# Second half's layer norm: convolution output turned through DRAM and VectorE instead of TensorE; first half's roots and turned blocks taken earlier

## The reference

```python
z = rmsnorm(x, g_mix) @ w_in            # a | b | v, 512 columns each
u = a * sigmoid(b)
u = causal_depthwise_conv(u, conv_w, conv_b)    # 31 taps, 512 channels
u = silu(layernorm(u, ln_g, ln_b))              # norm over the 512 channels
q = multiscale_pool(v, pool_w, pool_scale)
x = x + concatenate([u, q]) @ w_out
h = rmsnorm(x, g_ffn)                           # then SwiGLU FFN, gated embedding, rmsnorm
```

## Time and profile before

| | us |
|---|---|
| median of 3 runs (lowest, highest) | 990.74 (990.29, 991.52) |
| profiled execution, its own time | 991.45 |
| its span in the trace | 989.6 |
| TensorE busy | 976.5 |
| VectorE busy | 705.1 |
| ScalarE busy | 464.1 |
| GpSimd busy | 392.3 |

### The profile page before, as it was taken

One profiled execution on the slowest core, in us unless ns is written; L12 is line 12 of the kernel. 1 busy time (PEld: TensorE's weight loads), 2 busy tenths in 40 slices (PEclk: granted clock), 3 DMA queues, 4 the chain that ended last, 5 costly groups with the idle time before them and its releaser, 6 DMA issues.

```text
span 989.6 us, 12306 instructions
## 1 busy us (share of the span) xinstructions
PE 976.5 (99%) x4415; PEld 809.3 (82%) x4415; DVE 705.1 (71%) x984; ACT 464.1 (47%) x714; POOL 392.3 (40%) x297
## 2 busy tenths in 40 slices
PE   8999999999999999999999999999999999999996
PEld 7888887888888888888888888888888888888885
DVE  6999989976798365355354454553677888887897
ACT  6726357414364333333423333333444665676865
POOL 3467887920255544544444354451000000012555
PEclk9999999999999999999999999999999999999998
DMA  7631654476625134134233332413999688657432
GB/s 258 139 94 67 125 100 171 169 192 168 194 65 160 54 120 141 58 110 123 87 107 98 116 107 76 137 64 107 352 366 330 238 300 273 193 162 197 152 107 106
DMA packets 175663, 152.94 MB, mean 155 GB/s; under 512 B 73274, under 2 KB 131154, under 8 KB 175602
## 3 DMA queue, kind: packets, MB, share of 16 engines
q1 hardware_dynamic: 174400, 151.76, 49.8%
q10 hardware_dynamic: 1202, 0.40, 0.2%
HBM read 112.02 MB, written 40.11 MB: 154 GB/s over the span
## 4 chain that ended last, share of the span: by engine, by line
PE 81%; DVE 12%; POOL 2%; DMA 2%; ACT 1%; issue 1%; SPq 0%; POOLq 0%; DVEq 0%; ACTq 0%
PE ps L1758 27%; PE ps L1760 27%; PE ps L1759 27%; DVE ps L2226 8%; DMA raw<-in_w_in 2%; PE ps L1809 1%; POOL wide L956 1%; POOL ws_lo L849 0%; DVE resid L2234 0%; DVE resid L2226 0%; DVE ftmp L2655 0%; DVE act_lo L2119 0%; ACT junk L1135 0%; DVE scr L2147 0%; DVE ws_lo L2119 0%
## 5 line engine op out<-in xcount | busy, mean ns | idle before, releaser
L843 POOL TENSOR_SCALAR ss<-ss 128x1 f32<-128x1 f32 x38 | 15.6, 409 | 314.1 <-ACT junk L1135 278.6
L2226 DVE SCALAR_TENSOR_TENSOR ps<-resid,convw,ps 128x512 f32<-128x512 f32 x184 | 123.3, 748 | 0.0
L1758 PE MATMUL ps<-ring_hi,ring_lo 128*128 128x512 f32 x308 | 119.9, 389 | 0.1
L1760 PE MATMUL ps<-ring_hi 128*128 128x512 f32 x308 | 119.8, 389 | 0.0
L1759 PE MATMUL ps<-ring_lo,ring_hi 128*128 128x512 f32 x308 | 119.8, 389 | 0.0
L1758 PE MATMUL ps<-act_hi,bs_lo 128*128 128x512 f32 x240 | 93.5, 389 | 0.0
L1760 PE MATMUL ps<-act_hi,bs_hi 128*128 128x512 f32 x240 | 93.4, 389 | 0.0
L1759 PE MATMUL ps<-act_lo,bs_hi 128*128 128x512 f32 x240 | 93.4, 389 | 0.0
L2421 DVE TENSOR_TENSOR gtmp<-ps,gtmp 128x512 f32<-128x512 f32 x22 | 15.2, 691 | 95.6 <-PE ps L1760 95.6
L1121 ACT ACTIVATE ring_hi<-raw 128x512 fp32r<-128x512 f32 x89 | 51.9, 625 | 60.4 <-PE ps L1760 60.3
L849 POOL TENSOR_TENSOR wc_lo<-raw_b,wc_hi 128x1024 fp32r<-128x1024 f32 x22 | 55.7, 2530 | 48.8 <-ACT wc_hi L1121 47.7
(11 more groups left out here) (293 smaller groups left out, 2668.4 us busy)
## 6 DMA issues: line engine op xcount, KB each, us to landing
raw<-in_w_gate_up SPq DMA_DIRECT2D x44, 512.0 KB, 5.3
raw<-in_scratch SPq DMA_DIRECT2D x52, 256.0 KB, 3.6
raw<-in_w_down SPq DMA_DIRECT2D x52, 256.0 KB, 4.2
in_scratch<-in_s SPq DMA_DIRECT2D x44, 256.0 KB, 3.4
in_scratch<-gtmp SPq DMA_DIRECT2D x33, 256.0 KB, 2.3
keep<-in_w_down SPq DMA_DIRECT2D x32, 256.0 KB, 4.3
keep<-in_scratch SPq DMA_DIRECT2D x25, 256.0 KB, 3.4
resid<-in_x SPq DMA_DIRECT2D x8, 512.0 KB, 7.3
```

Source lines behind the costliest of these rows:

```text
L843: pool.tensor_scalar(ss[:, n:n + 1], ss[:, n:n + 1], 1.0 / D, EPS, ALU.mult, ALU.add)\
L1758: pe.matmul(dst, w_lo_, m_hi, start=start, stop=False, skip_group_check=onto)
L1760: return pe.matmul(dst, w_hi_, m_hi, start=False, stop=stop, skip_group_check=onto)
L2226: dve.scalar_tensor_tensor(out=conv_c if k == last_odd else acc, in0=u_all[:, c, k + h * BANK:k + (h + 1) * BANK], scalar=convw[:, c * 32 ...
```

## The change

The second half takes the first half's way to its layer norm: each chunk is stored to a second scratch tensor, loaded back by blocks, and turned by VectorE (`ln_turn_1`); TensorE's `conv_turn` is gone. The way back (`normed_turn` on TensorE) stays. In SP's queue four stores and eight loads stand between `load_quad(0)` and `store_x1(0)`. VectorE does statistics and scaling two tiles at a time, with `add_x(2)` in between, and scales only when all four tiles are turned, since the scaled tiles overwrite the loaded blocks. In the first half GpSimd takes the roots of tiles 0 and 1 behind the first addition of a window instead of the third, and VectorE's turns of the second pair of normed parts move from unit 6 into unit 5; the low parts `q_low` stand one tap later.

```diff
@@ SP
+            def store_conv_1(j):
+                c = UNIT_C[j]
+                sp.wait_ge(taps_done, ops_before(j + 1))
+                sp.dma_start(conv_dram_1.rearrange("(t c p) n -> c p t n", c=KC, p=P)[c],
+                             conv_o[:, c, BANK:2 * BANK].rearrange("p (t n) -> p t n", t=HT_LN)).then_inc(ln_stored, DMA)
+
+            for j in range(KC, 2 * KC):
+                store_conv_1(j)
+            sp.wait_ge(ln_stored, (2 * KC + HT_LN) * DMA)
+            load_ln(conv_dram_1, 0)
+            load_ln(conv_dram_1, 1)
@@ GpSimd
-                    if (s, j) == (0, 2):
+                    if (s, j) == (0, 0):
                         ln_rs(0, 2)
...
-            ln_rs(HT, TT)
+            ln_rs(HT, HT + 2)
+            ln_rs(HT + 2, TT)
@@ TensorE
-            def conv_turn(t):
-                for c in range(KC):
-                    ins = pe.transpose(ps[:, LN_BANK[t // HT][t % HT], c * P:(c + 1) * P],
-                                       conv_o[:, c, t * P:(t + 1) * P], ident[:, :])
-                ins.then_inc(lnf_mm, 1)
...
-            pe.wait_ge(taps_done, TAPS_ALL)
-            pe.wait_ge(taps_sum, 2 * KC - 1)
-            conv_turn(4)
-            conv_turn(5)
-            pe.wait_ge(rows_added, 2)
-            conv_turn(6)
-            conv_turn(7)
@@ VectorE
             def ln_scale(tiles):
                 for t in tiles:
                     dve.wait_ge(lrs_ok, HT_LN + t + 1)
+                    dve.wait_ge(ln_turned, KC + TT)
...
+            def ln_turn_1(t):
+                dve.wait_ge(ln_in[t // 2 - HT_LN // 2], 3 * DMA * (P // SQ))
+                dve.transpose(ps[:, LN_BANK[1][t - HT_LN], :], ln_part(t - HT_LN)).then_inc(ln_turned, 1)
...
+            def mixed_0_normed():
+                mix_low_0()
+                normed_second()
...
-            convolve(5, {14: normed_first, 25: mix_low_0})
-            convolve(6, {2: normed_second, 6: mix_low_2, 12: lambda: q_low(0), 16: lambda: q_low(1),
-                         20: lambda: q_low(2), 24: lambda: q_low(3)})
+            convolve(5, {14: normed_first, 26: mixed_0_normed})
+            convolve(6, {6: mix_low_2, 13: lambda: q_low(0), 17: lambda: q_low(1),
+                         21: lambda: q_low(2), 25: lambda: q_low(3)})
...
-            ln_stats(range(HT, TT))
-            ln_scale(range(HT, TT))
+            ln_turn_1(4)
+            ln_turn_1(5)
+            ln_stats(range(4, 6))
             add_x(2)
+            ln_turn_1(6)
+            ln_turn_1(7)
+            ln_scale(range(4, 6))
+            ln_stats(range(6, 8))
+            ln_scale(range(6, 8))
             add_x(3)
```

More of the change, by code:

```diff
@@ L77, in hybrid_block @@
     conv_dram = nc.dram_tensor("conv_scratch", (HT_LN * C, P), F32, kind="Internal").ap()
+    conv_dram_1 = nc.dram_tensor("conv_scratch_1", (HT_LN * C, P), F32, kind="Internal").ap()
     ln_dram = nc.dram_tensor("ln_scratch", (KC * BANK, P), F32, kind="Internal").ap()
@@ L261, in hybrid_block @@
         q_lo_ok = sem("q_lo_ok")
-        lnf_mm = sem("lnf_mm")
         ln_stored = sem("ln_stored")
@@ L2239, in ln_stats @@
                 for t in tiles:
[L2240 to L2243, removed]
+                    dve.wait_ge(ln_turned, t + 1 if t < HT_LN else KC + t + 1)
                     dve.bn_stats(bst[:, t, :], ps[:, LN_BANK[t // HT][t % HT], :]).then_inc(stats_ok, 1)
```

## The result

The changed kernel takes 992.37 us (median of 12 runs) against 990.95 us for the kernel before (12 runs): ratio 1.0016, 95% interval 1.0009 to 1.0023. It is 1.4 us slower, where 1.0 us faster was forecast. That is within the 0.2% that I called the same, but on the other side, and 0.4 us above the range. The profiled execution of the changed kernel took 991.55 us, the fastest of its twelve, with a span of 989.7 us.

The account below looks back on a forecast made before the run. TensorE was taken as the bound, busy 976.5 of 989.6 us. Gap -1.4, transposes -1.75, wait for scaled tiles +1.3 and later waits +0.85 gave -1.0 us: 989.7 against the median 990.74, range 987.6 to 992.0.

Parts of the forecast that it names:

- First half: Earlier roots and normed turns: TensorE 1.4 us earlier, VectorE's 2.35 us wait gone and its convolution ending 2.0 us earlier.
- The gap: TensorE's wait near 161 us for ScalarE's copy of an embedding product, 1.36 us lost, to close in full.
- The rival in which the first half gives nothing: Another ScalarE operation holds the copy and the gap stays: 991.8 us, within 0.2%; chance 0.15.
- The transposes: TensorE's 16 transposes of `conv_turn` before the second half's layer norm go, gaining 1.75 us.
- My floor of -3.15: Largest forecast gain on TensorE, from 212 us on: -1.4 for the gap and -1.75 for the transposes, 987.6 us.
- L: Time when SP begins the second half's eight loads of blocks: taken as 207.5 us, range 205.2 to 210.9.
- It waits 1.3 us; S is now -1.8: TensorE waits 1.3 us for the second half's scaled tiles; S, its shift against before (negative is earlier), becomes -1.8 us.
- what comes later: Small TensorE waits about 260 to 268 us, at the turns of tiles 5 and 6, costing 0.85 us.
- signs of being wrong: L off by over 1.5 us, next norm's blocks landing far from L + 18.3, or TensorE waiting somewhere unnamed.
- What is queued behind: Next norm's first block turn slips 0.15 us to 225.8; with 1.1 us slack, TensorE's shift stays at -0.95 or later.
- The round trip holds TensorE: Rival: stores crawl at 141 GB/s, L = 210.9, 993.2 us; any loss from L = 208.45; chance 0.11.
- All of it is gained: Rival: stores land by themselves, L about 205.2, or VectorE's slack about 260 is larger: 987.6 us; chance 0.32.

Follow-up runs that it names:

- experiment 1: Kernel before with only the first half's edits (earlier roots, second normed turns in unit 5, low parts one tap later): 989.75 us, ratio 0.9981.
- experiment 2: Changed kernel plus ten unused products on TensorE before its wait for the scaled tiles: 991.93 us, ratio 1.0002.
- experiment 4: Changed kernel with the first quad's weights and the stores of units 4 and 5 moved earlier in SP's queue: 989.87 us, ratio 0.9984.
- 6: Kernel of experiment 4 with the stores of x1 for tiles 0 and 1 also moved behind the loads of the next norm's blocks: 988.21 us, ratio 0.9966.
- 5: Changed kernel with the first half's edits put back, leaving the second half's round trip alone: 994.94 us, ratio 1.0032.
- 3: Changed kernel with 12 of tile 4's useful products issued before TensorE's wait for the scaled tiles: 992.48 us, ratio 1.0010.
- 9: Changed kernel with only the stores of x1 for tiles 0 and 1 moved behind the loads of the next norm's blocks: 992.88 us, ratio 1.0014.
- 10: Changed kernel with ten unused products before the wait and the stores of x1 behind the next norm's block loads: 991.52 us, ratio 0.9999.
- 7: Changed kernel with five unused products before TensorE's wait for the scaled tiles: 992.69 us, ratio 1.0013.

## Why the prediction was wrong

**First half, right.** The gap closes, VectorE's wait goes, and the first half gives 1.7 to 1.8 us at the end (experiment 1). I had -1.4 on TensorE and -2.0 on VectorE. The 0.4 us that TensorE got beyond the forecast hide a part of the miss behind it. The rival in which the first half gives nothing falls with this.

**The transposes, right.** TensorE's last product before the turn back was at 224.62 in the trace before and is at 219.70: 4.92 us earlier. 1.31 of it are the start, 1.75 the transposes, and the 1.86 that are left go to the first half. My floor of -3.15 was in truth about -3.6.

**The round trip, mis-sized.** By the terms of the sum, counted from the first add (202.84 in the forecast): L was to be 4.7 us behind it and is 5.1, in the traces of other kernels with the same queue up to 5.6. The first blocks were to land 5.0 us after L; the turn starts 5.6 after it. VectorE's work from there to the last scaling was forecast at 10.7 us and takes 212.45 to 223.22, 10.8. TensorE came 0.7 us sooner after the first add than forecast. Together the wait of 1.3 us became 3.2.

**The term that failed.** "It waits 1.3 us; S is now -1.8": the wait was too short by 1.9 us, and it was priced at its length alone. Behind a wait of 3.2 us the clock falls and the matmuls are slow, 1.6 us more, a term that the sum had at nothing. With the measured values, and the forecast's in brackets, the sum is -1.8 (-1.4) for the first half, -1.75 (-1.75) for the transposes, +3.2 (+1.3) for the wait, +1.6 (0) for the clock and +0.1 (+0.85) for what comes later: +1.4 instead of -1.0. No row of before had a wait of that length in this stretch; the 1.2 us of the earlier trace rows left the clock alone, and I took that for all waits. The Trainium skill (TensorE: Matmul & The Clock Gate, Why this matters for your kernels) names idle gaps between bursts of matmuls as the cause of drops in mid-kernel. The trace agrees: 3.18 us of idle time, then 0.50 of full clock. I had weighed no rule on the clock, though a wait of this length was inside my own range of L: at 210.9 it would have been 4.7 us. None of the signs of being wrong that I had listed came up: L was off by 0.4 us, the blocks by 0.9, and TensorE met no wait at a place that I hadn't named.

**What is queued behind, right in kind, short in size.** The next norm's first blocks were to be turned 23.0 us after the first add, L + 18.3; they are turned at 24.3, L + 19.2, for 20.8 before. From there the slip is handed on as forecast: 249.28 - 201.74 = 47.54 against 44.27 before, 3.3 us, where the forecast had 2.1. Less the slack of 1.1 this allows a lag of 2.2 and no less, where the forecast had 1.0; with the clock held it is 2.43, with a wait of 0.38 us at just the place that was named (experiment 2). So even without the clock this trace leaves no gain: 2.4 - 1.8 is +0.6 us, not -1.0; by time, experiment 2 can't be told from the kernel before.

**The rivals.** "The round trip holds TensorE" is what happened, but not by its mechanism alone: its deciding point, L = 208.45 for any loss, lies 5.6 us behind the forecast's first add. The profiled execution reached 5.07 and lost all the same, since the clock and the later landing weren't in the rule. "All of it is gained" needed L = 205.2; that is 2.4 us behind the first add; experiment 4 had it 2.66 us after, and gained only what experiment 1 gained. I had both bounds move with L, so that an L of 205.2 would free TensorE of both. It did not quite: the stores of x1 had to leave the queue too (6 against 4). With that, about what the floor promised was measured: ratio 0.9966, -3.4 us (-4.7 to -2.1), and -2.8 us by the trace, against -3.15.

**The cause.** Shown by times: the part of the change that loses is the second half (5), and it loses by SP's queue (4 and 6 against the changed kernel). That it does so through two bounds on TensorE, the late scaled tiles with the clock behind them and the next norm's blocks, is shown by the traces' waits (2, 3, 9, 10); the times of 2 and 10 alone don't part them, their intervals overlap. The fallen clock slowed the matmuls by 1.6 us in the changed kernel's trace; how much of that is lost at the end is less sure, 0.7 us by the lags and 1.4 us by the ratios. Why L differs by 0.6 us between executions of the same queue stays open. The profiled execution of the changed kernel was the fastest of its twelve and had one of the earlier L; experiments 3, 5, 7 and 9, with the same queue up to these loads, had 5.6 us.

## What to carry to other kernels

Work taken from a full engine is gained only if what replaces it has room in the queue that it goes through: here 1.75 us of transposes were traded for 2 MB in a list with a megabyte of weights ahead that was first read some 60 us later, and a megabyte of stores behind that nobody yet waited for; moving these, and two of the stores, made the same trade pay. When a forecast puts a new wait on TensorE, price it at its length and once more with the clock at its lower level behind it. When two bounds lie within a microsecond of each other, lifting one shows little; look in the trace for the next before giving up the first.

## What the runs showed of the hardware

The granted clock stayed at 1.00 over waits of 0.9, 1.2 and 2.5 us of an otherwise full TensorE (experiment 2, before, experiments 3 and 7), and fell to 0.50 with waits of 3.2, 3.4 and 3.6 us (changed kernel, experiments 5 and 9). It fell at different moments: 1.2 us behind the end of the first (about 224.5), 0.8 us before the end of the second (about 224.9), and at the end of the third (about 224.8). The 16 transposes behind took 2.53, 3.68 and 3.60 us, where they take 1.9 to 2.0 at the upper level, and the clock was back 4.7, 6.1 and 3.3 us behind the end of the wait.

From the end of the last store's issue to the loads that waited for all four stores, 4.1 us passed behind weights, gain and three more stores (202.71 to 206.81), and 2.2 us with the weights and two stores gone from there (202.74 to 204.94 in experiment 4). The eight loads in pieces of 128 bytes took SP 5.6 to 5.8 us to issue in all these kernels.
